# Seven block products instead of eight in the second product of an FFN (one Trainium2 core)

## The chip, the cores and the metric

The kernel runs on one core of one Trainium2 chip. The metric is the device time of one execution in microseconds (us). Lower is better.

## The reference, cut to what matters

The reference is one block of a transformer-like model: hidden width D = 1024, 1024 tokens. The mixers (hyena, grouped-query attention, neighbourhood attention) come first. The change touches only what stands after them, the feed-forward network (FFN) and the last norm:

```python
def swiglu(h, w_in_ffn, w_out_ffn):
    g, u = jnp.split(h @ w_in_ffn, 2, axis=-1)
    return (jax.nn.silu(g) * u) @ w_out_ffn
...
xl = xl + gt2 * swiglu(modulate(rms_norm(xl, g_ffn[l]), sh2, sc2), w_ffn_in[l], w_ffn_out[l])
...
return rms_norm(xl, g_final)
```

The hidden width of the FFN is 2816, that is 22 blocks of 128. `w_ffn_in` is 1024 x 5632, `w_ffn_out` is 2816 x 1024, all in fp32. `gt2` is a vector over the 1024 output columns.

## The kernel before

Every fp32 operand of a large product is split into two fp16 numbers, a high part (`hi`) and the rest (`lo`). One product of a 128x128 block with a 128x512 block is then three matmuls: hi·hi, hi·lo, lo·hi. ScalarE (ACT) writes the high part (a copy or a scaled copy to fp16), VectorE (DVE) writes the rest (fp32 minus the high part). Four engines and the DMA queue of SyncE (SP) each run their own list of instructions in order; they meet at semaphores.

**The first product (FFN in).** The hidden blocks are handled two at a time, as 11 pairs. Pair 0 is computed plainly. Pairs 1 to 10 already use seven block products (Strassen's scheme over halves of the tokens, halves of the width of 1024, and the two hidden blocks): the 14 steps of `STEPS` are P1, P2 for hidden block b = 0 and 1, then P5, P6, P7, P3, P4 for both. `product` on TensorE (PE) is one step: 12 matmuls of 128x128 by 128x512. `RING` = 7 split weight blocks (`aS`) lie ready ahead of PE. For each pair:

- SP loads the weights of one hidden block of the pair after next with `load_fi`, two DMAs for b = 0 and two for b = 1, each after `blk_lo` says that DVE has split the P4 block of the pair before. That is in the loop at lines 692 to 696.
- GpSimd (POOL) makes four kinds of weight sums, eight instructions a pair (`weight_sum`, lines 797, 802, 805, 808).
- ACT and DVE split the weight blocks (`block_hi`, line 1550; `block_lo`, line 2093). Block n + 7 is split in step n.
- ACT copies partial sums out of PSUM into six fp32 buffers (`snap`, line 1586), DVE adds to them (`gate_sum`, `up_sum`, line 2134), ACT applies silu (line 1591), and DVE multiplies gate by up (`gated`, line 2154). This gives four results of 128x512 for a pair: two token halves (`which` = 0, 1) by two hidden blocks (b = 0, 1).
- Each of the four is split: `gated_hi` (ACT, line 1601) and `gated_lo` (DVE, line 2165) write it into `prodT`. `gated_lo(0, 1)` is done early in the next pair, the other three at the end of their own.

The order on each engine is written out by hand in `pair_steps` (ACT line 1654, DVE line 2227). On PE, P1 of block b in the next pair waits until `gated(0, b)` has read the bank (`fi_p`); P6 waits for the snap of P1, P7,b for the snap of P6,b; P4 waits for `up_sum`. A `snap` may not overwrite a buffer before the split of the result that still lies in it.

**The second product (FFN out).** `down` multiplies 22 hidden blocks by all 1024 output columns, for four tiles of 128 tokens and then for the other four. A chunk of weights is two hidden blocks of 128x1024 fp32 (1 MB), loaded by `load_fo`, multiplied by `gt2` on DVE (`fo_gate`, line 2263), split by ACT (line 1695) and DVE (line 2273), in two buffers. Each chunk is loaded and split twice, once for each half of the tokens. Then come the residual (`gate_out`, line 2279), the square (line 1701), the root on POOL (line 823), the scaling (line 2288) and the store of the row. The matmuls of both products are recorded at line 829, in the helper `mm`.

Of the kernel before, what the change touches and what calls it, by code (L numbers as in the profile page):

```python
# [14 lines left out]
P = 128  # L15
# [32 lines left out]
          + ["qkv"] * 6 + ["wo"] * 4 + ["fi"] * KF + ["fo"] * KF)  # L48
# [49 lines left out]
NPLAIN = 8  # L98

# [130 lines left out]
def build(nc, io, cst, out):  # L230
    ctx = ExitStack()
    with ctx:
# [5 lines left out]
        x1_kept = nc.dram_tensor("x1_rows", (P, NT, D), F32, kind="Internal").ap()  # L238

# [125 lines left out]
        foS = [f16(36, 2, 2, 1024), f16(44, 2, 2, 1024)]  # L365
        gfin = f32(20, D)
        osq = f32(24, D)
        x2 = f32(68, NT, D)
# [4 lines left out]
        prodT = f16(Z, 2, KF, S)  # L373

# [89 lines left out]
        x1_back = sem("x1_again_in")  # L464
# [14 lines left out]
        fo_used = sem("ffn_out_chunk_used")  # L479
        fo_x = sem("x2_summed")  # L480
        fo_gated = sem("ffn_out_chunk_gated")
        fo_mm = sem("ffn_out_product")
        fo_sq = sem("x2_squares")
        fo_ms = sem("x2_mean_square")
# [100 lines left out]
        def _(sp):  # L585
# [65 lines left out]
            for h in range(HN):  # L651
# [45 lines left out]
            c1 = chunk_index("fo", 0)  # L697

            def load_fo(s, k):
                sp.dma_start(f32(RAW(s), 2, D), w_fo[:, bass.ds(k, 2), :]).then_inc(raw_in[s], 16)  # L700

            for b in range(2):
                sp.wait_ge(blk_lo, steps_before(NPAIR - 1) + step_of("P4", b) + 1)
                load_fo(b, 2 * b)
            for m in range(2, 6):
                sp.wait_ge(split_lo, n_split(c1 + m - 2))
                load_fo(m % 2, 2 * m)
            sp.wait_ge(fi_mm, steps_before(NPAIR))
            for i in range(4):
                sp.dma_start(x2[:, 2 * i:2 * i + 2], x1_kept[:, 2 * i:2 * i + 2]).then_inc(x1_back, 16)  # L710
            with sp.Fori(0, 2) as it:
                for b in range(2):
                    sp.wait_ge(split_lo, it * 2 + n_split(c1 + 4 + b))
                    load_fo(b, it * 4 + 12 + 2 * b)
            sp.wait_ge(split_lo, n_split(c1 + 8))
            load_fo(0, 20)
            with sp.Fori(0, 5) as it:
                for b in range(2):
                    sp.wait_ge(split_lo, it * 2 + n_split(c1 + 11 + b - 2))
                    load_fo(1 - b, it * 4 + 2 * b)  # L720
            sp.wait_ge(split_lo, n_split(c1 + 19))
            load_fo(1, 20)
            for t in range(NT):
                sp.wait_ge(fo_y, t + 1)
                sp.dma_start(out_rows[:, t], x2[:, t]).then_inc(out_done, 16)
            sp.wait_ge(out_done, 16 * NT)
# [3 lines left out]
        def _(pool):  # L730
# [83 lines left out]
            for p in SUMS:  # L814
                for b in range(2):
                    weight_sum(p, b, 1, True)
            with pool.Fori(0, NPAIR - 2) as it:
# [3 lines left out]
            for t in range(NT):  # L821
                pool.wait_ge(fo_ms, t + 1)
# [4 lines left out]
        def _(pe):  # L827
# [439 lines left out]
            def down(k0, s, grp, start, stop):  # L1267
                for t in range(4):
# [1070 lines left out]
```

## Time and profile before

| | us |
|---|---|
| time, median of 3 runs | 1478.21 (1473.32 to 1479.45) |
| the profiled execution, its own time | 1472.13 |
| its span from first to last instruction | 1470.3 |
| PE busy | 1401.9 |
| DVE busy | 940.9 |
| ACT busy | 652.4 |
| POOL busy | 255.4 |
| TensorE clock granted, mean | 0.99 of full |

The span is what the profile covers; about 1.8 us lie around it. Busy times are sums over the instructions of an engine. The mean duration shown of one matmul is longer than its share of the time, because matmuls overlap in the array: for the rate, a stretch is divided by its count.

### The profile page before, as it was taken

How to read it: one execution, taken by the hardware profiler on the slowest of the kernel's cores; microseconds unless marked ns; L12 is line 12 of the kernel's file. 1: busy time of each engine (PE TensorE's matmuls, PEld its weight loads, DVE VectorE, ACT ScalarE, POOL GpSimd, SP SyncE). 2: the span in 40 equal slices, each digit the busy share in tenths (PEclk: the TensorE clock that was granted, in tenths of full speed). 3: DMA queues.
4: the chain of work that ended last, by engine and by line, in shares of the span. 5: the costliest groups of instructions: out<-in, count | busy, mean ns of one | idle time of the engine just before them, and what ended most of it. 6: DMA issues, size and time to landing. Idle time of an engine off the chain costs nothing.

```text
span 1470.3 us, 24408 instructions
## 1 busy us (share of the span) xinstructions
PE 1401.9 (95%) x8581; PEld 767.2 (52%) x8581; DVE 940.9 (64%) x1395; ACT 652.4 (44%) x1187; POOL 255.4 (17%) x165
## 2 busy tenths in 40 slices
PE   5999998988988899999999999999999999999997
PEld 0374664544456677777654544444444444444443
DVE  2677777475278899999643597566565566345534
ACT  0451103433478788888631544444444442112221
POOL 0000000134131380000000043333333330000001
PEclk9999999999989999999999999999999999999999
DMA  6846564030040020020011302222222223523341
GB/s 238 328 157 233 211 227 145 5 96 0 0 120 0 11 105 29 10 75 0 2 43 43 86 1 58 57 57 57 57 57 57 57 57 131 227 95 106 102 138 74
DMA packets 93055, 130.66 MB, mean 89 GB/s; under 512 B 15459, under 2 KB 68685, under 8 KB 90829
## 3 DMA queue, kind: packets, MB, share of 16 engines
q1 hardware_dynamic: 86731, 126.35, 26.1%
q10 hardware_dynamic: 6274, 3.63, 0.8%
q8 instruction: 32, 0.52, 0.2%
q14 instruction: 18, 0.15, 0.0%
HBM read 119.09 MB, written 10.89 MB: 88 GB/s over the span
## 4 chain that ended last, share of the span: by engine, by line
PE 81%; DVE 6%; issue 4%; ACT 3%; DMA 2%; POOL 2%; ACTq 1%; DVEq 0%; SPq 0%; POOLq 0%
PE PS L829 73%; PE PS L1095 7%; DMA arena<-in_w_mod 1%; POOL arena L747 1%; ACT arena L1493 1%; PE PS L902 1%; ACTq L1306 1%; PE PS L1036 1%; DMA arena<-in_w_ffn_in 1%; DMA arena<-in_hy_f_wout 1%; DVE arena L1733 1%; ACT arena L1483 0%; POOL arena L797 0%; DVE arena L1975 0%; DVE arena L1961 0%
## 5 line engine op out<-in xcount | busy, mean ns | idle before, releaser
L829 PE MATMUL PS<-arena 128*128 128x512 f16 (+6 forms) x7276 | 1277.9, 334 | 36.7 <-DMA arena<-in_hy_f_wout 9.2
L829 PEld LDWEIGHTS PS<-arena 128*128 128x128 f16 (+3 forms) x7276 | 637.4, 103 | 619.4 <-issue 63.5
L2093 DVE SCALAR_TENSOR_TENSOR arena<-arena 128x512 f16<-128x512 f32 x148 | 129.3, 879 | 119.9 <-ACT arena L1550 119.6
L2037 DVE SCALAR_TENSOR_TENSOR arena<-PS,arena 128x512 f16<-128x512 f32 (+2 forms) x256 | 140.0, 599 | 6.3 <-ACT arena L1493 4.3
L1493 ACT ACTIVATE arena<-PS 128x512 f16<-128x512 f32 (+2 forms) x256 | 118.6, 531 | 52.5 <-PE PS L1095 52.5
L1550 ACT ACTIVATE arena<-arena 128x512 f16<-128x512 f32 x140 | 85.2, 626 | 89.6 <-PE PS L829 43.1
L1095 PE MATMUL PS<-arena 128*128 128x128 f32 x864 | 116.0, 280 | 7.8 <-ACT arena L1483 7.6
L1483 ACT ACTIVATE arena<-PS,arena 128x1280 f32<-128x1280 f32 (+1 forms) x96 | 118.0, 1230 | 1.1
L1095 PEld LDWEIGHTS PS<-arena 128*128 128x128 f32 x864 | 93.9, 141 | 46.8 <-ACT arena L1483 46.0
L2273 DVE SCALAR_TENSOR_TENSOR arena<-arena 128x2048 f16<-128x2048 f32 x20 | 45.8, 2292 | 107.2 <-ACT arena L1695 107.2
L1695 ACT ACTIVATE arena<-arena 128x2048 f16<-128x2048 f32 x20 | 38.2, 1910 | 162.5 <-PE PS L829 150.8
L2029 DVE TENSOR_REDUCE arena<-PS 128x1 f32<-128x1280 f32 x64 | 95.5, 1492 | 22.9 <-PE PS L829 22.9
L797 POOL TENSOR_TENSOR arena<-arena 128x512 f32<-128x512 f32 x20 | 29.2, 1463 | 243.1 <-DMA arena<-in_w_ffn_in 204.2
L747 POOL TENSOR_TENSOR arena<-arena 128x2 f32<-128x2 f32 (+1 forms) x18 | 23.3, 1296 | 229.6 <-DVE arena L1941 229.6
L1586 ACT COPY arena<-PS 128x512 f32<-128x512 f32 x60 | 34.6, 579 | 52.9 <-PE PS L829 26.6
L823 POOL TENSOR_TENSOR arena<-arena 128x1 f32<-128x1 f32 x8 | 7.2, 913 | 260.9 <-DVE arena L2284 260.9
L2134 DVE TENSOR_TENSOR arena<-PS,arena 128x512 f32<-128x512 f32 x60 | 41.1, 686 | 17.8 <-PE PS L829 17.5
L2263 DVE TENSOR_TENSOR arena<-arena 128x2048 f32<-128x2048 f32 x22 | 50.2, 2284 | 0.0
L1983 DVE TENSOR_TENSOR arena<-arena 128x256 f16<-128x256 f32 (+1 forms) x36 | 22.2, 635 | 41.2 <-ACT arena L1420 41.2
L1601 ACT CAST arena<-arena 128x512 f32 (+1 forms) x44 | 26.2, 616 | 43.2 <-DVE arena L2154 40.8
L783 POOL TENSOR_TENSOR arena<-arena 128x512 f32<-128x512 f32 x8 | 10.2, 1272 | 173.0 <-ACT arena L1504 173.0
L762 POOL TENSOR_TENSOR arena<-arena 128x640 f32<-128x640 f32 x20 | 27.0, 1380 | 65.6 <-PE PS L829 43.0
(153 smaller groups left out, 1004.3 us busy)
## 6 DMA issues: line engine op xcount, KB each, us to landing
arena<-in_w_mod SPq DMA_DIRECT2D x24, 1024.0 KB, 6.0
arena<-in_w_ffn_in SPq DMA_DIRECT2D x44, 512.0 KB, 5.1
arena<-in_w_ffn_out SPq DMA_DIRECT2D x22, 1024.0 KB, 4.8
arena<-in_w_in SPq DMA_DIRECT2D x9, 1024.0 KB, 6.0
arena<-cst_fwd SPq DMA_DIRECT2D x8, 1024.0 KB, 5.0
arena<-in_x SPq DMA_DIRECT2D x2, 2048.0 KB, 17.4
arena<-cst_inv SPq DMA_DIRECT2D x4, 1024.0 KB, 6.1
arena<-in_w_out SPq DMA_DIRECT2D x4, 1024.0 KB, 6.2
```

The source lines that it names most:

```text
L829: return pe.matmul(out, lhsT, rhs, start=start, stop=stop, skip_group_check=True)
L1095: ins = pe.transpose(PSf[:, o:o + P], Pb[:, u.par, i], ident)
L1483: act.activation(flat(Pb[:, u.par, 0:w]), PSf[:, 1536 * u.par:1536 * u.par + w * P], ACT.Exp, bias=nmax[:, u.par:u.par + 1], accum_out=esu ...
L1493: act.activation(flat(PT[:, u.par, 0, t.start:t.stop]), PSf[:, o:o + len(t) * P], ACT.Copy, scale=PSC).then_inc(pt_hi, 1)
L1550: act.activation(aS[n % RING][:, 0], weight_block(p, b), ACT.Copy, scale=WS).then_inc(blk_hi, 1)
L1695: act.activation(flat(foS[s][:, 0]), f32(RAW(s), 2048), ACT.Copy, scale=WS).then_inc(split_hi, 1)
L2029: dve.tensor_reduce(nmax[:, u.par:u.par + 1], PSf[:, o:o + w], AX, ALU.max, negate=True)\
L2037: dve.scalar_tensor_tensor(flat(PT[:, u.par, 1, t.start:t.stop]), PSf[:, o:o + len(t) * P], PSC, flat(PT[:, u.par, 0, t.start:t.stop]), AL ...
L2093: dve.scalar_tensor_tensor(dst[:, 1], src, WS, dst[:, 0], ALU.mult, ALU.subtract).then_inc(blk_lo, 1)
L2134: dve.tensor_tensor(buf[b], psum, buf[b], ALU.add).then_inc(fi_sum, 1)
L2263: dve.tensor_tensor(w, w, gate2.unsqueeze(1).broadcast_to((P, 2, D)), ALU.mult).then_inc(fo_gated, 1)
L2273: dve.scalar_tensor_tensor(flat(foS[s][:, 1]), f32(RAW(s), 2048), WS, flat(foS[s][:, 0]), ALU.mult, ALU.subtract).then_inc(split_lo, 1)
```

## The change

The second product is made of seven block products too. The left matrix (tokens by hidden) is cut into token halves and into the two hidden blocks of each pair; the right one (hidden by columns) into the same hidden blocks (k and k + 11) and into halves of the columns.

- The pairing of hidden blocks in the first product changes from (2i, 2i+1) to (i, i+11).
- The seven left operands A11, A12, A22, S1, S2, S3, S4 are made during the first product: four new DVE subtractions or additions in a pair (`operand_sum`), and seven splits in place of four (`operand_hi` on ACT, `operand_lo` on DVE). A `snap` now waits for the sums and splits that still read its buffer.
- Three of the left operands (A22, S1, S4) don't fit. They are stored to DRAM in each pair (`keep_left` on SP) and loaded again in the second product (`load_left`, 2.9 MB each).
- One sum of weights, T2 = B22 - B12 + B11, is made by POOL in each pair (two instructions, `weight_t2`), from three loads, and stored.
- In SP's loop, the loads for T2, its store, the stores of the three operands and a wait for S4's split stand ahead of the pair's `load_fi`.
- The second product runs P1, P6, P2, P7, P5, P4, P3, each 11 blocks by 4 token tiles by 3 matmuls. The right blocks (128x512) come through 8 raw buffers and a ring of 12 split ones; in P7, P5 and P4 a block is a difference of two loads, subtracted on DVE (`right_lo`).
- The gate `gt2` is applied to the sums of products, not to the weights. The sums are taken out of PSUM by `read` on DVE.
- All loops of the second product are written out.

```diff
-            def gated_lo(which, b, pair):
-
-                dve.wait_ge(fi_hi, pair * 4 + 2 * (1 - which) + b + 1)
-                gated_rest(which, b, pair)
+            def operand_lo(name, pair):
+
+                n = OPERANDS.index(name)
+                dve.wait_ge(fi_hi, pair * 7 + n + 1)
+                dst = staged[KEPT_OUT.index(name)] if name in KEPT_OUT else left[name][:, pair]
+                dve.tensor_tensor(dst[:, 1], f_op[name], dst[:, 0], ALU.subtract).then_inc(fi_lo, 1)
...
             def pair_steps(pair, first=False, last=False):
                 block_lo(7, pair)
-                if not first:
-                    gated_lo(0, 1, pair - 1)
+                operand_lo("S3", pair - 1)
+                operand_lo("S1", pair - 1)
                 gate_sum(0, 0, pair)
                 block_lo(8, pair)
+                operand_lo("A12", pair - 1)
                 block_lo(9, pair)
                 gate_sum(0, 1, pair)
                 for n in range(3, NSTEP):
...
+                    if n in (4, 5):
+                        operand_lo(("S2", "S4")[n - 4], pair - 1)
                     if n == 12:
+                        operand_sum("S3", pair)
                         gated(1, 1, pair)
-                        gated_lo(1, 0, pair)
+                        operand_sum("S1", pair)
...
                     if n == 13:
-                        gated_lo(1, 1, pair)
-                        gated_lo(0, 0, pair)
+                        operand_lo("A22", pair)
+                        operand_lo("A11", pair)
+                        operand_sum("S2", pair)
+                        operand_sum("S4", pair)
```

ACT's list, with the new waits of `snap`:

```diff
-            def snap(p, b, pair, first=False):
+            def snap(p, b, pair):
 
                 act.wait_ge(fi_mm, steps_before(pair) + step_of(p, b) + 1)
...
+                if (p, b) == ("P1", 0):
+                    act.wait_ge(fi_op, (pair - 1) * 4 + OPERAND_SUMS.index("S2") + 1)
+                elif p == "P1" or (p, b) == ("P5", 0):
+                    act.wait_ge(fi_op, (pair - 1) * 4 + OPERAND_SUMS.index("S4") + 1)
+                last_read = {"P1": ("A11", "A12"), "P5": ("S2", "S4"), "P6": ("S3", "S1")}[p][b]
+                act.wait_ge(fi_lo, (pair - 1) * 7 + OPERANDS.index(last_read) + 1)
...
             def pair_steps(pair, first=False, last=False):
...
+                operand_hi("S3", pair - 1, first)
+                operand_hi("S1", pair - 1, first)
                 block_hi(7, pair)
+                snap("P1", 0, pair)
                 block_hi(8, pair)
-                snap("P1", 1, pair, first)
+                operand_hi("A12", pair - 1, first)
+                snap("P1", 1, pair)
                 silu(0, 0, pair)
                 block_hi(9, pair)
                 block_hi(10, pair)
                 silu(0, 1, pair)
+                operand_hi("S2", pair - 1, first)
                 block_hi(11, pair)
-                snap("P5", 0, pair, first)
+                operand_hi("S4", pair - 1, first)
+                snap("P5", 0, pair)
                 block_hi(12, pair)
                 for n in range(6, NSTEP):
                     if n == 6:
-                        snap("P5", 1, pair, first)
+                        snap("P5", 1, pair)
                     if n < 8:
-                        snap("P6", n - 6, pair, first)
+                        snap("P6", n - 6, pair)
```

SP and POOL in the loop over pairs, and the new second product on PE:

```diff
             with sp.Fori(0, NPAIR - 2) as it:
+                load_t2(it)
+                keep_t2(it)
+                keep_left(it)
+                sp.wait_ge(t2_out, it * 16 + 16)
                 for b in range(2):
 
                     sp.wait_ge(blk_lo, steps_before(it + 1) + step_of("P4", b) + 1)
-                    load_fi(it * 2 + 4 + b, b)
+                    load_fi(it + 2 + KQ * b, b)
...
             with pool.Fori(0, NPAIR - 2) as it:
+                own.enter(it, 1)
+                weight_t2(it)
                 for p in SUMS:
...
+                for part, other in ((0, 0), (0, 1), (1, 0)):
+                    ins = mm(PS[:, bank, :], lhs[:, k, part, t * P:t * P + P], foS[q % FO_RING][:, other, :],
+                             p in ("P1", "P6", "P5", "P4") and k == 0 and part + other == 0,
+                             p in ("P2", "P7", "P4", "P3") and k == KQ - 1 and part == 1)
...
+            for p in DOWN[:-1]:
+                for k in range(KQ):
+                    for t in range(4):
+                        ins = down(p, t, k)
```

`right_lo` and `read` on DVE:

```diff
+                if len(RIGHT[p]) > 1:
+                    a, b = fo_raw[r % FO_RAW], fo_raw[(r + 1) % FO_RAW]
...
+                    dve.tensor_tensor(a, a, b, ALU.subtract).then_inc(fo_sum, 1)
+                    dve.wait_ge(fo_sum, down_sums(q) + 1)
+                dve.wait_ge(fo_hi, q + 1)
+                dve.scalar_tensor_tensor(foS[q % FO_RING][:, 1], fo_raw[r % FO_RAW], WS, foS[q % FO_RING][:, 0],
+                                         ALU.mult, ALU.subtract).then_inc(fo_lo, 1)
...
+                if p in ("P6", "P5", "P4"):
+                    dve.tensor_tensor(otmp[t % 2], bank, u_keep[:, t], ALU.add).then_inc(fo_read, 1)
+                    dve.wait_ge(fo_read, n_read)
+                    add_gated({"P6": "C12", "P5": "C22", "P4": "C21"}[p], t, otmp[t % 2], p != "P4")
```

## Rows read from the trace of the kernel before

**Rows 1.** Page: busy times, then lines of the chain that ended last.
```profile
PE 1401.9 (95%) x8581; PEld 767.2 (52%) x8581; DVE 940.9 (64%) x1395; ACT 652.4 (44%) x1187; POOL 255.4 (17%) x165
PE 81%; DVE 6%; issue 4%; ACT 3%; DMA 2%; POOL 2%; ACTq 1%; DVEq 0%; SPq 0%; POOLq 0%
```

**Rows 2.** By stretch (PE, PEld, DVE, ACT, POOL; clock, DMA share, GB/s): FFN in, FFN out.
```profile
905.00:1231.00 326.00, 325.25 (x1507) 147.47 (x1508) 198.78 (x251) 145.62 (x248) 102.08 (x67) 1.00 0.22 58
1236.00:1461.00 225.00, 224.72 (x1042) 101.78 (x1041) 105.46 (x61) 45.92 (x34) 4.13 (x6) 1.00 0.34 119
```

**Rows 3.** Timeline of PE: start, us, count, idle time before and its releaser.
```profile
887.93 15.70 PE L829 MATMUL PS<-arena 128*128 128x512 f16 x72 [0.64 <-DVE arena L2093]
905.75 329.10 PE L829 MATMUL PS<-arena 128*128 128x512 f16 x1524 [2.12 <-DVE arena L2154]
1235.76 4.49 PE L829 MATMUL PS<-arena 128*128 128x512 f16 x20 [0.91 <-DVE arena L2154]
```

**Rows 4.** Timeline of DVE in one pair, from the last gate sum on.
```profile
1118.41 0.69 DVE L2134 TENSOR_TENSOR arena<-PS,arena 128x512 f32<-128x512 f32 x1 [1.30 <-PE PS L829]
1119.94 1.75 DVE L2093 SCALAR_TENSOR_TENSOR arena<-arena 128x512 f16<-128x512 f32 x1
1121.61 0.68 DVE L2154 SCALAR_TENSOR_TENSOR arena<-PS,arena 128x512 f32<-128x512 f32 x1
1123.29 1.75 DVE L2154 SCALAR_TENSOR_TENSOR arena<-arena 128x512 f32<-128x512 f32 x1
1124.97 0.68 DVE L2165 TENSOR_TENSOR arena<-arena 128x512 f32 x1
1125.57 0.68 DVE L2154 SCALAR_TENSOR_TENSOR arena<-PS,arena 128x512 f32<-128x512 f32 x1
```

**Rows 5.** Timeline of DVE (block 12 of the pair), timeline of SP (the pair's loads).
```profile
1103.46 0.69 DVE L2093 SCALAR_TENSOR_TENSOR arena<-arena 128x512 f16<-128x512 f32 x1 [1.90 <-ACT arena L1550]
1104.35 76.57 SPq L679 DMA_DIRECT2D arena<-in_w_ffn_in  x12
```

**Rows 6.** DMA issues of the FFN out stretch: size, us to landing.
```profile
arena<-in_w_ffn_out SPq DMA_DIRECT2D x20, 1024.0 KB, 4.8
```

**Rows 7.** Chain at the end of the kernel: start, us, what.
```profile
1461.76 1.22 DVE arena L2279
1463.12 1.53 POOL arena L823
1464.68 1.28 DVE arena L2288
```

**Rows 8.** Groups from 950 to 1200: busy, mean ns, idle before.
```profile
L1591 ACT ACTIVATE arena<-arena 128x512 f32<-128x512 f32 x28 | 17.7, 630 | 5.4 <-DVE arena L2134 5.4
L1601 ACT CAST arena<-arena 128x512 f32 x27 | 16.0, 617 | 28.6 <-DVE arena L2154 28.6
L2134 DVE TENSOR_TENSOR arena<-PS,arena 128x512 f32<-128x512 f32 x42 | 28.8, 686 | 10.8 <-PE PS L829 10.5
```

**Rows 9.** Timeline of ACT in the pair of rows 4.
```profile
1092.44 0.58 ACT L1586 COPY arena<-PS 128x512 f32<-128x512 f32 x1 [1.96 <-DVE arena L2165]
1105.39 0.58 ACT L1586 COPY arena<-PS 128x512 f32<-128x512 f32 x1 [1.49 <-PE PS L829]
1110.09 1.15 ACT L1550 ACTIVATE arena<-arena 128x512 f16<-128x512 f32 x2 [1.53 <-DMA arena<-in_w_ffn_in]
```

**Rows 10.** Timeline of DVE between pairs 1 and 2.
```profile
908.36 1.76 DVE L2165 TENSOR_TENSOR arena<-arena 128x512 f16<-128x512 f32 x1
```

**Rows 11.** Timeline of POOL in the pair of rows 4.
```profile
1110.15 1.27 POOL L797 TENSOR_TENSOR arena<-arena 128x512 f32<-128x512 f32 x1 [22.04 <-DMA arena<-in_w_ffn_in]
1114.73 3.50 POOL L802 TENSOR_TENSOR arena<-arena 128x512 f32<-128x512 f32 x2
1121.10 3.39 POOL L808 TENSOR_TENSOR arena<-arena 128x512 f32<-128x512 f32 x2
```

**Rows 12.** Chain between pairs 1 and 2: start, us, what.
```profile
890.12 8.04 DMA arena<-in_w_ffn_in
898.16 0.02 issue
```

More of the change, by code:

```diff
@@ L98, with down_loads, down_sums @@
 NPLAIN = 8
+KQ = KF // 2
+OPERANDS = ("A22", "A11", "S3", "S1", "A12", "S2", "S4")
+OPERAND_SUMS = ("S3", "S1", "S2", "S4")
+KEPT_OUT = ("A22", "S1", "S4")
+DOWN = ("P1", "P6", "P2", "P7", "P5", "P4", "P3")
+LEFT = {"P1": "A11", "P6": "S2", "P2": "A12", "P7": "S3", "P5": "S1", "P4": "A22", "P3": "S4"}
+RIGHT = {"P1": ("B11",), "P6": ("T2",), "P2": ("B21",), "P7": ("B22", "B12"), "P5": ("B12", "B11"),
+         "P4": ("B21", "T2"), "P3": ("B22",)}
+DOWN_STEPS = [(p, k) for p in DOWN for k in range(KQ)]
+FO_RAW, FO_RING = 8, 12
+def down_loads(q):
+    return sum(len(RIGHT[p]) for p, _ in DOWN_STEPS[:q])
+def down_sums(q):
+    return sum(len(RIGHT[p]) > 1 for p, _ in DOWN_STEPS[:q])
 def steps_before(pair):
@@ L372, in build @@
         up2 = [f32(104, 512), f32(106, 512)]
-        prodT = f16(Z, 2, KF, S)
+        left = {n: f16(o, KQ, 2, 512) for n, o in (("A11", Z), ("S2", Z + 22), ("A12", Z + 44), ("S3", Z + 66),
+                                                   ("S1", 52), ("A22", 74), ("S4", Z))}
+        staged = [hT[:, :, i, 512:1024] for i in range(3)]
+        f_op = {"A11": gated1[0], "A12": gated1[1], "S3": gated2[0], "S1": gated2[1], "S2": up2[0], "S4": up2[1],
+                "A21": up2[0], "A22": up2[1]}
+        t2_in = [f32(Z + 91, 2, 256), f32(Z + 93, 2, 256), f32(68, 2, 16, 256)[:, :, 7]]
         first_in = sem("first_small_in")
@@ L715, in _ @@
[L715 to L725, printed above, removed]
@@ L729, in _ @@
+            sp.wait_ge(out_done, 16 * 2 * NT)
         @block.gpsimd
@@ L1724, in _ @@
+            for n in range(1, len(DOWN)):
+                for q in range(KQ * n, KQ * n + KQ):
+                    right_hi(q)
+                if n == 1:
+                    for t in range(4):
+                        act.wait_ge(fo_mm, t + 1)
+                        act.copy(u_keep[:, t], PS[:, 4 + t]).then_inc(fo_snap, 1)
+            for half in (1, 0):
+                for t in range(4):
+                    for d in range(2):
+                        x2_square(half, d, t)
         @block.vector
@@ L2317, in _ @@
-            mean_out(NT - 1)
-            norm_out(NT - 2)
-            norm_out(NT - 1)
+                    norm_out(1, t - 1)
+            norm_out(1, 3)
+            for t in range(4):
+                read("P3", t)
+                half_mean(0, t)
+                mean_out(0, t)
+                if t:
+                    norm_out(0, t - 1)
+            norm_out(0, 3)
 INPUTS = ["x", "c", "ctx", "c_ctx", "w_mod", "b_mod", "g_mix", "g_ffn", "w_in", "w_out", "hy_conv_w", "hy_conv_b",
```

463 lines of the change are left out of this document (281 added, 182 removed).

## The prediction

> **What bounds the kernel now.** I read the page's busy times and chain first: PE is busy 95% of the span and carries 81% of the chain [rows 1]. Then busy time by stretch: in both halves of the FFN, PE is busy for practically the whole stretch, while DVE has 199 of 326 us and 105 of 225 us [rows 2]. So both are bound by the number of matmuls. The rate comes from counts: 329.10 us for 1524 matmuls and 225.00 for 1042 both give 0.216 us each [rows 2, 3]. One step (12 matmuls) is 2.59 us, one pair (14 steps) 36.28 us. PE waits only three times, for 0.64, 2.12 and 0.91 us: the first two between pairs 1 and 2, the third where the second product begins [rows 3]. The reader should see that DVE has slack in the sum; what has to be checked is whether it has slack in its order.
>
> **What the second product saves.** Before: 22 blocks x 8 token tiles x 2 column halves x 3 = 1056 matmuls. After: 7 products x 11 blocks x 4 tiles x 3 = 924. 132 fewer, x 0.216 = 28.5 us off. All of it lies on the path, if the blocks arrive in time. The wait of 0.91 us for the last `gated` at the seam also goes [rows 3], because P1 now goes into banks that are free: 29.4 us off together.
>
> Do the blocks arrive? One block feeds PE for 12 matmuls, 2.59 us. *DVE:* in P7, P5, P4 a block costs a subtraction, ACT's copy and the rest in turn: 0.69 + 0.63 + 0.60 and two hand-overs, about 2.0 us, since an SBUF operation alone takes 0.69 and follows another at 0.60 [rows 4, 5]. Eleven are 22 us. `read` adds up to 4 tiles x 3 dependent operations x 0.72 = 8.6 us, for the product before. In the worst product that is 30.6 us against 28.5, but the one before it needs 24.5, and a ring of 12 is almost one product of cover. I take 0, at most 2. *DMA:* two 256 KB loads in 2.59 us are 200 GB/s; a 1 MB load lands in 4.8 us today, 218 GB/s at one load at a time [rows 6]. The three operands of 2.9 MB are asked for one or two products before their use. I take 0; the bound from above is one such load uncovered, 2.9 MB at 218 GB/s, 13 us. *Tail:* the last row costs two additions of 0.7 in place of one of 1.22, a shorter square, the same root and scaling [rows 7]: within 0.5 us of today, taken as 0.
>
> **What the first product pays.** Per pair the change adds on DVE four sums and three more splits, on ACT three casts (0.62 each [rows 8]), on POOL two instructions, and on SP seven DMAs. In the sum this is small: DVE 22 us of 36, plus 7 x 0.6 to 1.7. But the added instructions stand in a chain that returns to itself, in order lists: landing of a pair's weights -> DVE's list to the last `gated` -> the splits of operands -> `snap`s and silus -> split of S4 -> SP's `load_fi`, which now stands behind that split -> landing of the next weights. Before, the load left at 1104.35, right after block 12 was split (1103.46 + 0.69) [rows 5], and the weights landed at 1110.09 [rows 9]. I walk the new loop with 0 = landing of the first half of the weights:
>
> - 0 to 6.4: blocks 14 to 17, two up sums, two gate sums begun. Before, this ended 8.3 us after the landing, of which at least 1.30 was a wait for PE at the last gate sum [rows 4, 9], 0.5 a shorter one.
> - 6.4 to 17.0: from the last gate sum to the end of the last `gated`. Before: 1118.41 to 1126.25, 7.8 us [rows 4]. Out goes `gated_lo(1, 0)` (0.6 [rows 4]), in come S3 and S1. While POOL is working, a DVE operation with two SBUF inputs that follows such another one takes 1.75 us in place of 0.69 (and 1.67 until the next), a subtraction too: 1.76 [rows 4, 10]; one with a PSUM input keeps its 0.68 [rows 4, 8]. POOL works back to back here from 1114.73 to 1124.49 [rows 11], and two instructions for T2 now follow. So S3 and S1 cost 1.7 each, not 0.6: 7.8 - 0.6 + 3.4 = 10.6.
> - 17.0 to 25.1: block 20 (1.1), then ten at 0.6 to 0.8, 7.0 together: splits of A22 and A11, sums S2 and S4 (each waits for the one before), block 7, splits of S3 and S1, gate sum, block 8, split of A12. POOL ends near 18.
> - 25.1 to 28.1: the snap of P1,1 may now overwrite its buffer only after A12's split: ACT 0.5 + silu 0.54 (its 0.63 overlaps the next [rows 8]) + cast 0.63, DVE 0.6 + 0.7. Today the snap of P1,0 waits for such a split too, 1.96 us at 1092.44, but far from PE's need [rows 9].
> - 28.1 to 33.6: ACT silu, S2 cast, block 11 (1.7); DVE block 11 and the split of S2 (1.3), for which the snap of P5,0 waits; ACT 0.5 + 0.63; DVE block 12 and the split of S4 (1.3).
> - 33.6 to about 40: SP stores S4 and then issues the loads; landing as today 5.9 after the release, and something for the store ahead of it.
>
> That is 38.8 to 40.3 us for a pair that PE can do in 36.28. I take 39.8: 3.5 us of PE idle per pair. Two waits of PE would show it: P1,1 of the next pair (due 5.2 us into the pair) waits for `gated(0, 1)`, about 4 us; then P7,0 waits for the snap of P6,0, which ACT reaches at 34.1, up to 2 us. Today that snap is taken as soon as P6,0 ends, at 1105.39 [rows 9]. The loop runs from the load of pair 2 to that of pair 10, 8 periods: 28 us.
>
> The first round is dearer. Between pairs 1 and 2 PE already waits for this load (landing at 898.16 after 8.04 us [rows 12]; idle 2.12 [rows 3]), so nothing covers a later start. Eleven DVE operations come in before that load (four sums, seven splits, some of them contended), one split goes, and ACT's new waits stand between them: about 9 us until the load, about 1 more behind it. I take 10 (5 to 13). The last pair has the wait at P7,0 alone: 2. Sum: 28 + 10 + 2 = 40 us (bounds: 8 x 1.5 + 5 = 17 below, 8 x 4.5 + 13 + 3 = 52 above, where the landing takes 1 us more and every contended operation its full 1.7).
>
> What is the rule behind the 1.7 us? The rows show that DVE's operation begins when POOL's ends, and POOL's takes 1.70 in place of 1.27 [rows 11]. The Trainium skill, SBUF — State Buffer, section "SBUF: two separate sides", says that VectorE and GpSimd share one port pair under an exclusive lock, where the loser fully blocks. The trace agrees: 1.75 is one POOL instruction of about 1.15 and one DVE instruction of 0.6. If they shared bandwidth and POOL only slowed DVE by a share, S3 and S1 would cost 1 us less each, and the loop would lose some 2 of its 3.5 us.
>
> **Sum.** 1472.1 (the profiled execution) - 29.4 + 40 = 1483. The median of the runs shown, 1478.2, is 6.1 above the profiled execution; I forecast the median, so 1478.2 + 10.6 = 1489 us. About 0.5% (7.4 us) is what a measurement can tell from no change.
>
> **Rivals.**
> 1. *The loop stays hidden, the saving arrives.* For: DVE's busy sum would be about 29 of 36 us, and today's chain has 8.3 us from landing to the last gate sum where it needs 6.4. Against: the list above has 39 to 40 us of dependent links. It decides at 36.3 us per pair: below that only the first round costs (0 to 10). Time: 1478.2 - 29.4 + 0 to 10 = 1449 to 1459. Faster.
> 2. *The loop is a little over.* At 37.5 to 38.5 a pair (S3 or S1 falls into a gap of POOL, SP issues at once) the price is 8 x 1.7 + 10 + 1 = 25: 1474, between 1459 and 1482.
> 3. *The second product starves too*, on top of the forecast: one 2.9 MB operand is late or the double loads don't keep pace, 5 to 13 us more: 1495 to 1503.
> 4. *The change doesn't do what it says.* The count of 924 follows from the loops, so only the rate could fail: a product of 132 matmuls would take more than its 28.5 us. That is rival 3 again, and it has no chance of its own.
>
> **How the numbers follow.** Forecast 1489 (1482 to 1495): 0.50. Rival 2: 0.27. Rival 1: 0.15. Rival 3: 0.08. Faster by over 0.5% (under 1470.8): all of rival 1 and a quarter of rival 2, 0.22. Within 0.5% (to 1485.6): the rest of rival 2 and a little of the forecast, 0.25. Slower: 0.53. The range leaves out rival 1 and the top of rival 3: 1459 to 1500.
>
> **What would show it.** Right: between pairs, PE idle in two places, with DVE L2154's `gated` and ACT's `snap` as releasers, and some 40 us in all between 905 and the second product; loads of `w_ffn_in` some 39 to 40 us apart; the second product's 924 matmuls in about 200 us with next to no wait; DVE's subtractions S3 and S1 at 1.7 us beside POOL. Wrong: pairs 36.3 us apart (the loop has slack that I counted away, above all in the order between ACT and DVE), sums S3 and S1 at 0.7 us, or PE idle in the second product for `right_lo` or a kept operand.

## The result, and the profile after

The changed kernel takes 1494.94 us (median of 4 runs, 1491.18 to 1497.47), the kernel before 1476.18 beside it (4 runs, 1473.32 to 1479.45). The ratio is 1.0124, with a 95% interval of 1.0091 to 1.0157: slower by 1.2%. The profiled execution of after took 1491.18 us, its span 1489.4 against 1470.3 before.

**The busy times** (page of after; engine, busy us, share of the span, instructions) have to be read beside [rows 1]:

```profile
PE 1382.7 (93%) x8449; PEld 752.6 (51%) x8449; DVE 1017.7 (68%) x1602; ACT 673.2 (45%) x1295; POOL 292.5 (20%) x187
```

The 132 matmuls are gone (8581 to 8449) and no other engine is near its limit, and yet the span grew by 19.1 us. **By stretch** (the columns of [rows 2]: PE, PEld, DVE, ACT, POOL; clock, DMA share, GB/s), the first round, then the steady part of FFN in, then FFN out, then the 28.5 us of it in which the DMA engines are busiest:

```profile
882.00:929.00 47.00, 36.11 (x146) 14.84 (x145) 34.00 (x39) 17.48 (x32) 20.65 (x13) 0.89 0.32 94
929.00:1282.00 353.00, 321.89 (x1473) 141.95 (x1472) 246.51 (x307) 148.69 (x273) 127.00 (x80) 1.00 0.34 99
1282.00:1482.00 200.00, 199.83 (x926) 90.41 (x924) 123.02 (x199) 61.25 (x113) 8.47 (x9) 1.00 0.64 225
1310.80:1339.30 28.50, 28.50 (x134) 12.91 (x133) 10.03 (x16) 9.60 (x17) 0.00 (x0) 1.00 0.96 379
```

PE is idle for 31 of 353 us in FFN in, where it was idle for 0.75 of 326 [rows 2], and for 0.2 of 200 in FFN out. **The timeline of PE** (columns of [rows 3]) shows where:

```profile
841.86 42.25 PE L948 MATMUL PS<-arena 128*128 128x512 f16 x195
...
886.47 4.28 PE L948 MATMUL PS<-arena 128*128 128x512 f16 x12 [2.37 <-issue]
891.78 2.75 PE L948 MATMUL PS<-arena 128*128 128x512 f16 x12 [1.03 <-issue]
900.89 23.71 PE L948 MATMUL PS<-arena 128*128 128x512 f16 x96 [6.36 <-issue]
925.74 15.70 PE L948 MATMUL PS<-arena 128*128 128x512 f16 x72 [1.13 <-DVE arena L2282]
...
1087.88 15.70 PE L948 MATMUL PS<-arena 128*128 128x512 f16 x72 [1.44 <-DVE arena L2282]
1104.66 15.71 PE L948 MATMUL PS<-arena 128*128 128x512 f16 x72 [1.08 <-ACT arena L1705]
1121.56 5.35 PE L948 MATMUL PS<-arena 128*128 128x512 f16 x24 [1.19 <-DVE arena L2282]
1128.35 15.70 PE L948 MATMUL PS<-arena 128*128 128x512 f16 x72 [1.43 <-DVE arena L2282]
...
1249.70 15.70 PE L948 MATMUL PS<-arena 128*128 128x512 f16 x72 [1.44 <-DVE arena L2282]
1266.69 215.14 PE L948 MATMUL PS<-arena 128*128 128x512 f16 x996 [1.29 <-ACT arena L1705]
```

Count matmuls to see which step waits. The pieces of a pair are 24, 72 and 72: PE waits ahead of P1,0 (for `gated(0, 0)`, L2282), ahead of P1,1 (for `gated(0, 1)`) and ahead of P7,0 (for the snap of P6,0, L1705). From pair to pair it takes 1128.35 - 1087.88 = 40.47 us, and on average (1249.70 - 925.74) / 8 = 40.50. Without waits it is 36.28. The three idle times add up to 3.7 us; the other 0.5 of the 4.2 us lost lies in the three fresh starts, since 24, 72 and 72 matmuls take 5.35, 15.70 and 15.71 us where 0.216 each would be 5.18, 15.55 and 15.55. The last piece runs from P7,0 of the last pair to the end of the second product without a wait: the second product starts at 1282.23 (1266.69 and 72 matmuls) and ends at 1481.83, 199.6 us.

**The account of the time.** One thing has to be taken out first. The long row of PE with which this part of the kernel starts begins at 841.86 here and in the kernel before at

```profile
839.87 47.43 PE L829 MATMUL PS<-arena 128*128 128x512 f16 x219
```

that is 2.0 us earlier, in a part that the change doesn't touch. In the profiled executions of the eleven kernels of this document this start moves by up to 8.2 us, so I measure from it. From the start of that row to the end of the span: 630.4 before, 647.5 after, +17.1 us.

| part | before | after | |
|---|---|---|---|
| up to the long row | 839.9 | 841.9 | +2.0 |
| from there to P1,1 of pair 2 | 71.1 | 83.9 | +12.8 |
| 8 periods, P1,1 of pair 2 to that of pair 10 | 290.2 | 324.0 | +33.7 |
| last pair, the wait at P7,0 | | 1.3 | +1.3 |
| second product, with the seam | 229.5 | 199.6 | -29.9 |
| tail | 8.6 | 7.6 | -1.0 |

The sum is +18.9, the spans differ by 19.1. (P1,1 of pair 2 before: 905.75 of [rows 3] and 24 matmuls, 910.95.)

### The profile page after: what moved, and what is told of

Its sections match the earlier page's. It is cut to its first block and busy times, and to the rows that moved or that the text cites. A ratio compares the mean times of both kernels' runs of the same rounds, so it can differ in the third digit from the quotient of the medians.

```text
span 1489.4 us, 24717 instructions
## 1 busy us (share of the span) xinstructions
PE 1382.7 (93%) x8449; PEld 752.6 (51%) x8449; DVE 1017.7 (68%) x1602; ACT 673.2 (45%) x1295; POOL 292.5 (20%) x187
## 5 line engine op out<-in xcount | busy, mean ns | idle before, releaser
L948 PE MATMUL PS<-arena 128*128 128x512 f16 (+6 forms) x7144 | 1260.3, 334 | 75.5 <-DVE arena L2282 22.3
L948 PEld LDWEIGHTS PS<-arena 128*128 128x128 f16 (+3 forms) x7144 | 623.9, 103 | 653.9 <-issue 99.8
L2221 DVE SCALAR_TENSOR_TENSOR arena<-arena 128x512 f16<-128x512 f32 x148 | 134.3, 913 | 113.2 <-ACT arena L1669 113.2
L1669 ACT ACTIVATE arena<-arena 128x512 f16<-128x512 f32 x140 | 84.4, 624 | 74.2 <-DMA arena<-in_w_ffn_in 67.2
L1783 ACT ACTIVATE arena<-arena 128x512 f16<-128x512 f32 x77 | 48.2, 628 | 121.2 <-DVE arena L2376 64.8
L2379 DVE SCALAR_TENSOR_TENSOR arena<-arena 128x512 f16<-128x512 f32 x77 | 52.9, 697 | 66.5 <-ACT arena L1783 66.5
L1733 ACT CAST arena<-arena 128x512 f16<-128x512 f32 (+1 forms) x77 | 44.8, 608 | 66.7 <-DVE arena L2282 62.1
L853 POOL TENSOR_TENSOR arena<-arena 128x2 f32<-128x2 f32 (+1 forms) x18 | 23.3, 1296 | 229.5 <-DVE arena L2069 229.5
L1705 ACT COPY arena<-PS 128x512 f32<-128x512 f32 x60 | 34.2, 587 | 72.5 <-DVE arena L2296 50.4
L2296 DVE TENSOR_TENSOR arena<-arena 128x512 f16<-128x512 f32 (+1 forms) x77 | 53.9, 724 | 0.0
```

Of the source, the lines that this page charges most:

```text
L948: return pe.matmul(out, lhsT, rhs, start=start, stop=stop, skip_group_check=True)
L1669: act.activation(aS[n % RING][:, 0], weight_block(p, b), ACT.Copy, scale=WS).then_inc(blk_hi, 1)
L1733: act.copy(dst, f_op[name]).then_inc(fi_hi, 1)
L1783: act.activation(foS[q % FO_RING][:, 0], fo_raw[r % FO_RAW], ACT.Copy, scale=WS).then_inc(fo_hi, 1)
L2221: dve.scalar_tensor_tensor(dst[:, 1], src, WS, dst[:, 0], ALU.mult, ALU.subtract).then_inc(blk_lo, 1)
L2296: dve.tensor_tensor(dst[:, 1], f_op[name], dst[:, 0], ALU.subtract).then_inc(fi_lo, 1)
```

## The experiments

The first theory is that of the prediction: the order of the lists makes a loop that is longer than a pair. Its rivals: the work or the port that DVE and POOL share, the new traffic, and the second product. Each kernel is the one after with one thing changed, or e4 with one thing more where that is said. Here they are together, in us; "rest" is from the start of the long row to the end of the span, "first round" from there to P1,1 of pair 2, as in the account. It is blank for e6, where P1,1 of pair 2 lies inside a longer row.

| kernel | time (runs) | long row starts | rest | first round | a pair |
|---|---|---|---|---|---|
| before | 1476.18 (4) | 839.87 | 630.4 | 71.1 | 36.28 |
| after | 1494.94 (4) | 841.86 | 647.5 | 83.9 | 40.50 |
| e1_loads_before_s4 | 1480.06 (1) | 845.85 | 632.5 | 82.2 | 38.88 |
| e2_small_t2 | 1480.72 (1) | 840.02 | 638.9 | 81.1 | 39.75 |
| e3_s2_s4_early | 1461.89 (4) | 843.97 | 616.1 | 79.7 | 37.28 |
| e6_gated_only | 1498.31 (1) | 846.35 | 650.2 | | 40.6 |
| e4_gated_before_sums | 1452.23 (5) | 841.00 | 609.1 | 77.9 | 36.63 |
| e5_double_stores | 1496.15 (1) | 842.07 | 652.3 | 84.5 | 41.0 |
| e7_first_round | 1457.28 (4) | 848.06 | 607.8 | 77.8 | 36.48 |
| e8_t2_in_gap | 1449.18 (5) | 842.82 | 604.0 | 75.7 | 36.28 |
| e9_t2_gap_alone | 1486.62 (1) | 847.78 | 637.0 | 80.5 | 39.5 |

The start of the long row follows TensorE's granted clock in the mixers, far ahead of the change. Busy times by stretch (columns as above) of e2_small_t2, which starts it at 840.02:

```profile
200.00:300.00 100.00, 95.37 (x477) 52.72 (x476) 61.44 (x148) 34.32 (x75) 9.16 (x11) 0.98 0.33 111
```

and of e7_first_round, which starts it at 848.06:

```profile
200.00:300.00 100.00, 95.36 (x453) 53.70 (x452) 59.27 (x142) 31.09 (x71) 7.51 (x10) 0.93 0.32 108
```

PE is busy equally long, at a clock of 0.93 instead of 0.98, and gets 24 matmuls less done. The next 100 us are at 0.95 and 0.98. All eleven kernels fall into this order: clocks of 0.98 and 0.98 in the two stretches go with starts of 839.87 and 840.02, 0.98 and 0.95 with 841.00 to 842.07, 0.97 and 0.95 with 842.82 and 843.97, 0.93 and 0.98 with 845.85, 0.93 and 0.95 with 846.35 to 848.06. Why the clock differs there is not known. A single time is therefore good to some 8 us. "Rest" and "a pair" are free of that. How well they repeat is not shown, since each kernel has one profile; the last row of PE, 996 matmuls, takes 215.14 us in after, e1, e2, e5 and e9 and 216.83 in e6.

### SP: the store of S4 behind the loads

```diff
-                keep_left(it)
+                keep_left(it, KEPT_OUT[:2])
...
                     load_fi(it + 2 + KQ * b, b)
+                keep_left(it, KEPT_OUT[2:])
```

> The store of S4 stands behind the two load_fi in SP's loop; nothing is left out. Theory (the weights' load waits for S4's split, and this closes the loop that sets 40.5 us a pair): the first half's load leaves 1.5 us earlier (block 12 is split at 1102.9, S4 at 1103.5 and SP issues at 1104.4), the second half's load still waits for block 13; pairs 38.9 us apart (38.0 to 39.5), time 10 to 18 us less. Rival 1 (PE's own waits for gated and snap set the pair, the load only follows): pairs stay at 40.3 to 40.5. Rival 2 (the added DMA traffic makes the weights late): the traffic is the same, so 40.3 to 40.5 too.

Pairs take 38.88 us, by the timeline of PE. SP (columns: start, us, queue, line, count) in after, and then in this kernel:

```profile
1089.58 14.46 SPq L762 DMA_DIRECT2D left_operands<-arena  x3
1104.41 3.92 SPq L730 DMA_DIRECT2D arena<-in_w_ffn_in  x4
```

```profile
1084.85 4.17 SPq L764 DMA_DIRECT2D left_operands<-arena  x2
1098.34 3.96 SPq L730 DMA_DIRECT2D arena<-in_w_ffn_in  x4
1102.55 1.36 SPq L764 DMA_DIRECT2D left_operands<-arena  x1
```

After P1,1 (1087.88 and 1083.14) the loads leave at 16.5 us in after and at 15.2 here. One store moved, nothing removed, 1.6 us a pair back: the place of the load in SP's list is a link of the loop. It isn't the only one, since 38.88 is still 2.6 over PE's need.

### POOL: T2's two instructions made short, which leaves out 511 of T2's 512 columns

```diff
+                a, b, c = (v[:, 0, 0:1] for v in t2_in)
-                own.step(pool.tensor_tensor(t2_in[1], t2_in[0], t2_in[1], ALU.subtract))
+                own.step(pool.tensor_tensor(b, a, b, ALU.subtract))
                 own.wait()
-                pool.tensor_tensor(t2_in[0], t2_in[1], t2_in[2], ALU.add).then_inc(t2_rdy, 1)
+                pool.tensor_tensor(a, b, c, ALU.add).then_inc(t2_rdy, 1)
```

> POOL makes T2 for one column only instead of 512; the rest of T2 is left out, all waits and DMAs stay. It prices the port contention of the two new POOL instructions. Theory: S1's sum falls from 1.65 to 0.7 us and block 20's split from 1.15 to 0.7, both are on the loop, pairs 1.3 to 1.6 us shorter (39.0), time about 13 us less. Rival (POOL is off the path, DVE has 11 us of idle time in a pair to take it): pairs stay at 40.5 within 0.3 us.

Pairs take 39.75 us: 0.75 less, half of what I expected. The timeline of DVE, after first:

```profile
1122.50 1.75 DVE L2303 TENSOR_TENSOR arena<-arena 128x512 f32<-128x512 f32 x1
1124.17 1.75 DVE L2282 SCALAR_TENSOR_TENSOR arena<-arena 128x512 f32<-128x512 f32 x1
1125.95 1.65 DVE L2305 TENSOR_TENSOR arena<-arena 128x512 f32<-128x512 f32 x1
1127.52 0.68 DVE L2282 SCALAR_TENSOR_TENSOR arena<-PS,arena 128x512 f32<-128x512 f32 x1
1128.12 1.15 DVE L2221 SCALAR_TENSOR_TENSOR arena<-arena 128x512 f16<-128x512 f32 x1
```

```profile
1118.39 0.69 DVE L2306 TENSOR_TENSOR arena<-arena 128x512 f32<-128x512 f32 x1
1119.00 0.68 DVE L2283 SCALAR_TENSOR_TENSOR arena<-PS,arena 128x512 f32<-128x512 f32 x1
1120.17 0.69 DVE L2222 SCALAR_TENSOR_TENSOR arena<-arena 128x512 f16<-128x512 f32 x1 [0.49 <-ACT arena L1670]
```

The sum for S1 fell from 1.65 to 0.69 as said, and the wait at P1,1 fell by the same 0.96 (1.44 to 0.48). But DVE's next instruction, the split of block 20, now waits 0.49 for ACT's cast (L1670), so the splits behind it come 0.85 us earlier and not the 1.4 us that the two shorter instructions give (from the start of the sum to the end of that split it takes 2.47 us instead of 3.32). The port is a part of the price, not the cause of the loop.

### ACT and DVE: S2 and S4 split right after A12

```diff
                 operand_hi("A12", pair - 1, first)
-                snap("P1", 1, pair)
-                silu(0, 0, pair)
+                operand_hi("S2", pair - 1, first)
+                operand_hi("S4", pair - 1, first)
                 block_hi(9, pair)
+                silu(0, 0, pair)
+                snap("P1", 1, pair)
                 block_hi(10, pair)
                 silu(0, 1, pair)
-                operand_hi("S2", pair - 1, first)
                 block_hi(11, pair)
-                operand_hi("S4", pair - 1, first)
                 snap("P5", 0, pair)
```

and on DVE `operand_lo("S2")` and `operand_lo("S4")` right behind `operand_lo("A12")`.

> Only the order changes: casts and splits of S2 and S4 come directly after A12's, and block 9's cast and silu come before the snap of P1,1. Same instructions, same stores. Theory (the loss is the order, not the work): S4's split no longer waits for silu, block 11 and the snap of P5,0, block 12 is split about 1.9 us earlier and the load leaves 3.5 us earlier; PE's wait for the snap of P6,0 goes; pairs 37.0 us apart (36.6 to 37.8), time 28 to 36 us less, 1460 to 1466. Rival (DVE and ACT are simply too full with the new work): pairs 40.0 to 40.5, no change.

The time is 1461.89 us, a ratio to before of 0.9904 (0.9869 to 0.9939). In PE's timeline one short wait a pair is left:

```profile
1110.32 36.42 PE L948 MATMUL PS<-arena 128*128 128x512 f16 x168 [0.77 <-DVE arena L2282]
```

After P1,1 of a pair (1073.13) the loads now leave at 12.1 us (1085.27) instead of 16.5. Every instruction of the change is still there, on every engine, and so is every byte; 31.4 us (647.5 - 616.1) of the 33.7 + 1.3 + 12.8 that the first product had lost are back. That is the order and nothing else: with the old order ACT's snaps waited for splits that stood behind ACT's own casts, which stood behind the snaps.

### DVE: `gated(0, 1)` ahead of the sums S3 and S1, alone and on top of the last

```diff
-                    if n in (12, 13):
-                        gated(0, n - 12, pair)
+                    if n == 12:
+                        gated(0, 0, pair)
...
                     if n == 12:
-                        operand_sum("S3", pair)
                         gated(1, 1, pair)
+                        gated(0, 1, pair)
+                        operand_sum("S3", pair)
                         operand_sum("S1", pair)
```

> Only gated(0, 1) moves ahead of the sums S3 and S1 on DVE, so P1,1 no longer waits for it. Theory (one loop through the weights' load): that wait of PE, 1.43 us a pair, goes, but S4's split is where it was, so the idle time moves to other waits and pairs stay 40.2 to 40.6 us apart; time within 4 us. Rival (each of PE's three waits is a cost of its own): 1.4 us a pair less, 39.1, time 13 us less.

> The order of e3_s2_s4_early, and gated(0, 1) ahead of the sums S3 and S1. Same instructions. Theory (with S4's split early, the load's loop is under PE's 36.28 us, and P1,1's wait for gated is the only one left, 0.68 to 1.1 us a pair): now this order pays what it didn't pay in e6_gated_only: pairs 36.3 to 36.5 us apart, time 7 to 9 us under e3_s2_s4_early, about 1453, and faster than the kernel before by about 23 us. Rival (the load's loop is still over PE's pace and only shows as this wait): pairs stay at 37.0 to 37.3, time as e3_s2_s4_early.

Alone, on after, it takes away the wait that it is aimed at, and the pair stays at 40.6 us. PE's timeline, and then a stretch (columns as above) right behind a later wait of 2.69 us at P7,0:

```profile
1068.98 15.71 PE L948 MATMUL PS<-arena 128*128 128x512 f16 x72 [2.68 <-ACT arena L1705]
1085.87 20.89 PE L948 MATMUL PS<-arena 128*128 128x512 f16 x96 [1.18 <-DVE arena L2282]
```

```profile
1150.20:1154.00 3.80, 3.79 (x11) 1.48 (x12) 0.69 (x1) 0.95 (x2) 0.00 (x0) 0.59 0.93 261
```

The 1.44 us at P1,1 came back at P7,0, 1.08 there having become 2.7. That is how a loop behaves: its length is fixed elsewhere, and the idle time only moves along it. From 1109 on a second thing shows it: behind each wait at P7,0 the clock falls for a few microseconds (0.59 above), the 168 matmuls of a pair take some 38 us instead of 36.4, the wait at P1,0 is gone, and the pair is still 40.6 us long. On top of the last experiment, where the loop has been cut, the same edit gives its 0.6 us a pair: 36.63 us, 1452.23 us, ratio 0.9834 (0.9819 to 0.9848).

### SP: the stores doubled

```diff
-                    sp.dma_start(left_kept[i][...], staged[i]).then_inc(left_out[i], 16)
+                    for kept in (left_kept, left_again):
+                        sp.dma_start(kept[i][...], staged[i]).then_inc(left_out[i], 16)
```

> The changed kernel with each store of A22, S1 and S4 made twice, to two places in DRAM: 0.75 MB a pair more. Theory (the loss is the order of the lists; of the traffic only what stands directly ahead of the load counts): S4's second store costs its issue and its own transfer, 0.3 to 0.8 us a pair, time 3 to 7 us more. Rival (the added DMA traffic, stores above all, makes the weights late): the pair has 1.5 MB of stores and loads of its own for 4.2 us of loss, 0.75 MB more cost about 2 us a pair, time 16 us more or worse.

A pair takes 41.0 us instead of 40.5, so a second set of stores costs 0.5 us, and the rest grows by 4.8 us. The traffic itself doesn't explain 4.2 us a pair. What its first set costs alone wasn't tried, but e3 carries it at 37.28 us a pair.

### DVE: the first round in another order, on top of e4

```diff
             operand_sum("S2", 0, True)
+            block_lo(6, 1)
             operand_sum("S4", 0, True)
...
                 gate_sum(0, 0, pair)
-                block_lo(8, pair)
                 operand_lo("A12", pair - 1)
+                block_lo(8, pair)
```

> e4_gated_before_sums with another order in the first round: pair 0's splits of A22 and A11 and the sum S2 ahead of block 6, A12's split ahead of block 8. Theory (the first round's loss is PE waiting for the snaps of P1, behind S2 and A12's split, and then for the later load): P6,0 no longer waits 2.4 us, and 1 to 3 us of the rest go: time 2 to 4 us under e4_gated_before_sums. Rival (block 6 then comes late itself, or POOL's port sets the pace): no difference, or up to 1 us more.

This missed. The time is 1457.28 us (1450.65 to 1457.88), ratio 0.9844 (0.982 to 0.9868), which is no gain over e4; its long row started 7.1 us later, and the rest is 1.3 us shorter, of which the first round has 0.1. PE's timeline:

```profile
890.75 2.76 PE L948 MATMUL PS<-arena 128*128 128x512 f16 x12 [0.44 <-DVE arena L2221]
897.24 5.28 PE L948 MATMUL PS<-arena 128*128 128x512 f16 x12 [3.72 <-DVE arena L2221]
```

and ACT's snap of P1,1:

```profile
896.55 0.58 ACT L1705 COPY arena<-PS 128x512 f32<-128x512 f32 x1
```

The wait of 2.37 us at P6,0 fell to 0.44 us, and it is now for block 6 (L2221), which I had put behind the sum. The next step, P6,1, then waits 3.72 us. The profile names a split of DVE for it, but block 7, which that step reads, had been split at 894.04, and the step begins 0.11 us after the snap of P1,1 ends. That snap stands behind a silu in ACT's list, and DVE reaches the gate sum for that silu only at 895.17, behind a row of splits and sums of up to 1.75 us each beside a busy POOL.

### POOL: T2 in the gap ahead of the next weights

```diff
             with pool.Fori(0, NPAIR - 2) as it:
                 own.enter(it, 1)
+                pool.wait_ge(blk_lo, steps_before(it + 2))
                 weight_t2(it)
```

and on SP `keep_t2(it)` and `load_t2(it + 1)` behind the pair's `load_fi`. Once on top of e4, once on after alone.

> e4_gated_before_sums, and POOL makes T2 after the split of the pair's last block (block 13), while DVE waits 5.5 us for the next weights, instead of behind its weight sums beside DVE's busiest stretch; SP stores T2 behind load_fi. Same instructions. Theory (T2's two POOL instructions hold the port against S1's sum, block 20's split and, in the first round, a chain of six DVE operations): pairs go from 36.63 to 36.3 us, the first round gives 3 to 5 us, time 5 to 8 us under e4_gated_before_sums, 1444 to 1447. Rival (PE sets the pace by now, and the first round's loss is the snaps' waits alone): within 2 us of e4_gated_before_sums, 1450 to 1453.

> The changed kernel with T2 moved into the gap and nothing else. It repeats e2_small_t2 without leaving work out. Theory: S1's sum at 0.7 us, pairs 39.75 us apart as in e2_small_t2 (ACT's casts then hold block 20), the first round 4.7 us shorter: 10 to 11 us less than the changed kernel. Rival (e2_small_t2 was shorter because of less POOL work, not because of its place): within 3 us of the changed kernel.

On top of e4 the time is 1449.18 us (5 runs, 1448.57 to 1453.57), ratio to before 0.9812 (0.9794 to 0.9831): 1.9% faster than before, and the best kernel here. The gain over e4 was to be larger: 3 us in the medians, 5.1 in the rest. PE's timeline from pair 2 to the end is one row:

```profile
913.28 525.94 PE L949 MATMUL PS<-arena 128*128 128x512 f16 x2436 [0.23 <-DVE arena L2283]
```

Groups from 960 to 1240 (busy us, mean ns) in after, then in this kernel: DVE's sums S3 and S1 and POOL's two for T2.

```profile
L2303 DVE TENSOR_TENSOR arena<-arena 128x512 f32<-128x512 f32 x7 | 12.2, 1749 | 0.0
L926 POOL TENSOR_TENSOR arena<-arena 128x512 f32<-128x512 f32 x7 | 12.0, 1718 | 0.0
L2305 DVE TENSOR_TENSOR arena<-arena 128x512 f32<-128x512 f32 x7 | 11.5, 1648 | 0.2
L928 POOL TENSOR_TENSOR arena<-arena 128x512 f32<-128x512 f32 x7 | 11.2, 1601 | 0.5
```

```profile
L926 POOL TENSOR_TENSOR arena<-arena 128x512 f32<-128x512 f32 x9 | 11.9, 1318 | 163.9 <-DVE arena L2222 134.4 <-DMA arena<-in_w_ffn_out 29.5
L928 POOL TENSOR_TENSOR arena<-arena 128x512 f32<-128x512 f32 x9 | 12.1, 1339 | 0.7
L2306 DVE TENSOR_TENSOR arena<-arena 128x512 f32<-128x512 f32 x7 | 5.8, 832 | 0.0
L2304 DVE TENSOR_TENSOR arena<-arena 128x512 f32<-128x512 f32 x7 | 5.2, 744 | 0.0
```

Alone on after, the shift brought pairs of 39.5 us, as expected, and the rest fell by 10.5 us (647.5 to 637.0), also as expected. The span by itself would have said 4.6 and hidden it: that run's long row began at 847.78, 5.9 us later than after's.

The account closes from the other side too. From before to e8 the second product gives 29.9 and the tail 1.0, the first round costs 4.6, the pairs nothing: -26.3 us. The rest of the two differs by 604.0 - 630.4 = -26.4.

## Why the prediction was right, and where it was off

**Second product: right.** The forecast was -29.4 us, 199.6 against 229.5 us is -29.9, with 0.2 us of idle. Its DVE is busy for 123 of 200 us. In the busiest 28.5 us the DMA engines move 379 GB/s at a share of 0.96, about 10.8 MB, in which the kept operands and 256 KB blocks come together. The three operands of 2.9 MB land 11.5 to 18.0 us after their issue. The blocks issued in these 28.5 us have a median of 12.4 us to landing, against 4.1 over the whole product, and PE stays busy for 28.50 us of 28.50. Rival 3 falls. The tail gave 1.0 us where I had put 0.5 at most.

**The loop: the right mechanism, link by link.** I set the landing of the first half of the weights to 0. In after the first cast behind it is at 1110.49 (ACT's timeline), and a period before that at 1070.0:

```profile
1095.04 0.58 ACT L1705 COPY arena<-PS 128x512 f32<-128x512 f32 x1 [2.69 <-DVE arena L2296]
1101.06 0.58 ACT L1705 COPY arena<-PS 128x512 f32<-128x512 f32 x1 [0.85 <-DVE arena L2296]
1103.53 1.07 ACT L1705 COPY arena<-PS 128x512 f32<-128x512 f32 x2 [1.36 <-DVE arena L2296]
1110.49 1.15 ACT L1669 ACTIVATE arena<-arena 128x512 f16<-128x512 f32 x2 [4.88 <-DMA arena<-in_w_ffn_in]
```

| link | forecast | in after |
|---|---|---|
| last `gated` begins (1127.52 - 1110.49) and ends | ends 17.0 | 17.0, 17.7 |
| snap of P1,1, behind A12's split | 25.1 | 1095.04: 25.0 |
| snap of P5,0, behind the split of S2 | 31 | 1101.06: 31.1 |
| split of S4 done, snap of P5,1 and of P6,0 | 33.6 | 1103.53: 33.5 |
| load leaves | | 1104.41: 34.4 |
| landing | 39.8 | 40.5 |

Up to the split of S4 the walk is right to 0.1 or 0.7 us; the end of the last `gated` comes 0.7 later than forecast, and the list behind it, taken as 8.1 us, needs 7.3, so two small errors cancel. **The term that was mis-sized** is the last: from that split to the landing I took 6.2 us (today's 5.9 and something), and it is 7.0: 0.9 until SP has stored S4 and issued the load, and 6.1 for the load. A period is 0.7 us longer for it, and 8 of them are 5.7 us (33.7 against 28). My bound of 40.3 from the walk was still too low; the bound of the sum, 4.5 us a pair, held it.

**Where PE waits: partly wrong.** I named two waits, about 4 us at P1,1 and up to 2 at P7,0. There are three, of 1.2, 1.4 and 1.1 us: P1,0 waits for `gated(0, 0)` as well, which I had not followed. The idle sum is that of the loop, but where it lies is set by each step's own slack; e6 shows how freely it moves.

**The first round: right to 3 us, by another cause.** 12.8 us against 10 (bounds 5 to 13). I had said that the load of pair 2's weights would be late and nothing would cover it. The load is late (it leaves at 900.54, 58.7 us after the start of the long row; before the change at 887.79, 47.9 us after it), but PE's three long waits of 2.37, 1.03 and 6.36 us, at P6,0, P6,1 and P7,0, are for snaps; only the 1.13 us at P1,1 lie behind the load. The profile names no releaser for the three, but each of these steps begins 0.10 us after a snap has ended. ACT's timeline there:

```profile
885.79 0.58 ACT L1705 COPY arena<-PS 128x512 f32<-128x512 f32 x1 [4.65 <-DVE arena L2308]
891.10 0.58 ACT L1705 COPY arena<-PS 128x512 f32<-128x512 f32 x1 [3.69 <-DVE arena L2296]
899.72 1.07 ACT L1705 COPY arena<-PS 128x512 f32<-128x512 f32 x2 [1.42 <-DVE arena L2296]
```

The snap of P1,0 waits 4.65 us for the sum S2 (L2308). DVE's two splits ahead of it take 3.42 us and the sum itself 1.74 beside POOL's last weight sums and T2 (e8 and e9, where T2 is elsewhere, have 3.4 us less here against after and 2.2 less against e4). The idle times of the four rows add up to 10.9 us, and some 4 more are matmuls at a lower clock (next section). Before, 2.8 us stood in their place (0.64 and 2.12 [rows 3]). 15 - 2.8 is 12; the account has 12.8. That the sum came out near the forecast is in part luck.

**The port.** S3 and S1 took 1.75 and 1.65 us where I had 1.7, so their sizes were right. The rows don't show what I read from them, that DVE's operation begins when POOL's ends: the row of S1 begins at 1125.95, 1.10 us before POOL's first instruction for T2 ends (1127.05), and ends 0.55 after it. That its own work starts at 1127.05 is an inference; it fits the 0.6 us that such an operation takes alone. What was wrong was to think (in e2's expectation) that all of such a microsecond lies on the path. The Trainium skill, SBUF — State Buffer, section "Who interferes with whom", says that a DVE instruction with two SBUF inputs contends with a GpSimd instruction that reads SBUF, and that the one that comes second blocks until the first is through. The trace agrees on both sides: with T2 moved away POOL's own instructions fell from 1718 and 1601 to 1318 and 1339 ns, and DVE's from 1749 and 1648 to 744 and 832.

**The total.** I forecast +10.6 us, and the profiled executions differ by 19.1. The loop is 5.7 of the 8.5 us between them, the first round 2.8 and the start of the long row, which I had not reckoned with, 2.0; the last pair (1.3 where I had 2), the second product and the tail take back 2.2. The median of 1494.94 us lies just inside the forecast's band of 1482 to 1495. That it does is luck, since the start of the long row alone moves by more than the 0.06 us that were left.

**The medians.** The profiled execution of before was 6.1 us under the median then known, and I forecast the median by adding the same sum to it. The runs bear out that the two differ by the clock: executions of before with a mean clock of 0.990 have spans of 1471.3 to 1472.7 us, those with 0.985 have 1476.8 to 1478.5. By the profiles such a difference lies ahead of the long row.

**The rivals.** Rival 1 (hidden loop, 1449 to 1459) fell for this kernel, but it names what the same instructions can do in another order: e4 at 1452 and e8 at 1449. Rival 2 (37.5 to 38.5 us a pair, 1459 to 1482) is close to e3, with 37.28 us a pair and 1461.89.

**What stays open.** The first round still costs 4.6 us in e8, and e7 shows only that one wait there turns into a longer one at the next step; how its price divides between the snaps, POOL and the lower clock was not settled. The other cost of the three stores, their place in DMA queues, was measured only for a second set of them.

## What to carry to other kernels

Added instructions on an engine with slack are free in its sum and can cost their whole worth in its order: walk the chain from a load's landing through every list back to the next issue of that load, and compare its length with the period of the bound engine. Here that walk gave 39.8 us where 40.5 was measured, and cutting it (two splits moved a few places up in two lists) brought back 31 us, where an earlier load brought 15 and a shorter instruction on the shared port 9. When one wait is taken away and the period stays, the idle time has moved along a loop; look for the link where two engines wait for each other in turns.

## What the hardware showed that I had not expected

**The clock in the first round.** Granted clock by stretch in after: the first step behind the 2.37 us of idle, then the start of the piece behind the 6.36 us:

```profile
887.00:891.00 4.00, 3.75 (x12) 1.18 (x10) 3.99 (x7) 0.41 (x1) 0.00 (x0) 0.68 0.56 193
901.00:910.00 9.00, 9.00 (x30) 3.39 (x30) 3.72 (x5) 1.95 (x4) 1.27 (x1) 0.69 1.06 290
```

Before, 882 to 906 was at 1.00. PE was idle for 2.37, 1.03 and 6.36 us within 20 us, and in parts of what followed it was granted the lower of its two levels, 1.2 instead of 2.4 GHz: 96 matmuls took 23.71 us instead of 20.7 (96 x 0.216). The lower clock cost some 4 us on top of the 10.9 us of idle time. The later waits of 1.1 to 1.4 us in every pair cost nothing of that kind: the clock is 1.00 from 929 to 1282. The waits of 2.7 us in e6 are between the two: behind the first four, ahead of 1109, the clock stays at 0.99 to 1.00, behind those from 1109 on it falls to about 0.6 for some 4 us, which costs about 1.6 us a pair. What decides between the two was not settled.

**A part that the change doesn't touch moves a single time by 8 us.** In e9 it hid more than half of the gain: 4.6 us by the span, 10.5 from the long row on. A landmark in the trace right ahead of the changed part takes it out.
